# Early Sqrt table, identity on SyncE's queue, a first low part on VectorE, and a last tile squared and scaled in halves

## What is computed

```python
def _rmsnorm(x, g):
    xf = x.astype(jnp.float32)
    y = xf * lax.rsqrt(jnp.mean(xf * xf, axis=-1, keepdims=True) + EPS)
    return (y * g.astype(jnp.float32)).astype(x.dtype)
```

## Time and profile before

| | us |
|---|---|
| median of three runs (lowest, highest) | 1605.75 (1604.44, 1608.35) |
| the profiled execution | 1602.53 |
| its span (first to last instruction) | 1600.8 |

### The profile page before, as it was taken

How to read it: one execution, slowest core, us unless ns; L and a number is a source line. 1 busy time by engine, 2 the same in 40 slices (tenths; PEclk the granted TensorE clock), 3 DMA queues, 4 the chain that set the end, 5 groups by cost and what they waited for, 6 DMA issues and landing times.

```text
span 1600.8 us, 18917 instructions
## 1 busy us (share of the span) xinstructions
PE 1503.7 (94%) x7408; PEld 1009.0 (63%) x7409; DVE 662.9 (41%) x1092; ACT 512.8 (32%) x913; POOL 474.1 (30%) x250
## 2 busy tenths in 40 slices
PE   7999999999999999999998999899699998999996
PEld 6974567888788888888867766457334343433443
DVE  3156665223633333321135679573523233222234
ACT  5246566222543333321246333424111111111112
POOL 3441115444434444444424363432100000000000
PEclk9999999999999999999999999999799999999999
DMA  7333001232333233223223222217899999999995
GB/s 302 107 102 91 2 1 40 93 94 91 99 101 103 93 97 101 92 93 105 92 80 119 87 77 66 105 53 299 344 430 430 429 430 430 428 431 425 427 425 235
DMA packets 47272, 306.12 MB, mean 191 GB/s; under 512 B 6560, under 2 KB 6688, under 8 KB 33488
## 3 DMA queue, kind: packets, MB, share of 16 engines
q1 hardware_dynamic: 42256, 290.56, 47.1%
q0 software_dynamic: 4352, 12.25, 2.1%
q10 hardware_dynamic: 576, 2.10, 0.4%
HBM read 302.84 MB, written 4.19 MB: 192 GB/s over the span
## 4 chain that ended last, share of the span: by engine, by line
PE 74%; DMA 10%; DVE 9%; ACT 4%; issue 2%; POOL 0%; SPq 0%; DVEq 0%; ACTq 0%; POOLq 0%
PE banks L407 26%; PE banks L1090 11%; PE banks L437 10%; DMA ring<-experts 8%; PE banks L1121 4%; PE banks L2221 3%; PE banks L943 2%; PE banks L417 2%; PE banks L2150 2%; PE banks L1130 2%; PE banks L2166 2%; DMA arena<-experts 1%; PE banks L800 1%; PE banks L2133 1%; PE banks L801 1%
## 5 line engine op out<-in xcount | busy, mean ns | idle before, releaser
L370 POOL TENSOR_TENSOR arena_r<-ring,arena_r 128x1024 fp32r<-128x1024 f32 x143 | 352.2, 2468 | 444.5 <-ACT arena_r L355 444.5
L407 PE MATMUL banks<-hT_r,arena_r 128*128 128x512 f32 x1216 | 388.6, 391 | 5.5 <-POOL arena_r L370 4.3
L355 ACT ACTIVATE arena_r<-ring 128x1024 fp32r<-128x1024 f32 x143 | 150.6, 1059 | 461.3 <-PE banks L407 303.2
L407 PE MATMUL banks<-arena_r 128*128 128x512 f32 x800 | 291.7, 389 | 0.0
L407 PEld LDWEIGHTS banks<-hT_r,arena_r 128*128 128x128 f32 x1216 | 228.6, 188 | 59.5 <-issue 9.1
L1090 PE MATMUL banks<-ring,arena 128*64 128x512 f32 x720 | 223.3, 607 | 14.2 <-DMA ring<-experts 13.9
L437 PE MATMUL banks<-arena_r 128*128 128x512 f32 x784 | 184.1, 389 | 2.5 <-POOL arena_r L370 1.9
L407 PEld LDWEIGHTS banks<-arena_r 128*128 128x128 f32 x800 | 150.4, 188 | 31.0
L437 PEld LDWEIGHTS banks<-arena_r 128*128 128x128 f32 x784 | 147.0, 188 | 34.1 <-POOL arena_r L370 3.8
L1090 PEld LDWEIGHTS banks<-ring,arena 128*64 128x64 f32 x720 | 71.8, 140 | 149.5 <-issue 149.5
L1709 DVE TENSOR_TENSOR resid<-resid,banks 128x1024 f32<-128x1024 f32 x63 | 74.0, 1217 | 129.9 <-PE banks L1130 129.9
(11 more groups left out here) (443 smaller groups left out, 1896.6 us busy)
## 6 DMA issues: line engine op xcount, KB each, us to landing
arena<-experts SPq DMA_DIRECT2D x42, 2048.0 KB, 16.8
ring<-stream SPq DMA_DIRECT2D x162, 512.0 KB, 3.7
ring<-experts SPq DMA_DIRECT2D x37, 2048.0 KB, 16.5
ring<-experts SPq DMA_DIRECT2D x12, 1024.0 KB, 15.4
arena<-experts SPq DMA_DIRECT2D x12, 1024.0 KB, 16.7
ring<-experts SPq DMA_DIRECT2D x8, 512.0 KB, 12.3
resid<-x ACTq DMA_DIRECT2D x4, 512.0 KB, 5.6
grow<-grows POOLq DMA_DIRECT2D x4, 512.0 KB, 6.7
```

What stands on the lines that cost most here:

```text
L355: nc.scalar.activation(parts(name, m)[:, 0, :], tile(tile_n), ACT.Copy).then_inc(S["w_high"], 1)
L370: nc.gpsimd.tensor_tensor(w[:, 1, :], tile(tile_n), plain(w[:, 0, :]), ALU.subtract).then_inc(S["w_low"], 1)
L407: last = nc.tensor.matmul(pb[:, bank, :], w[:, a, k * P:(k + 1) * P], b[:, k, :], start=(k == 0 and part == 0), stop=(k == ND - 1 and part ...
```

## The change

Six edits. (1) VectorE sets a column to 1 at once, and ScalarE, after its four DMA issues, takes a Sqrt of it into an unused column. (2) The identity and eps are loaded by SP, as its first DMA, and counted with x tile 0 (`x_in0` reaches 32); SP issues W0 after x tile 2 (was tile 1), and after x tile 3 first `cols`, then W1; GpSimd no longer issues either. (3) The low part of W0 is made by VectorE; GpSimd waits for it and goes on with W1. (4) At n1 and n2, the last tile's square is shared: ScalarE squares the first 512 columns, VectorE squares and sums the other 512 (with eps added), and the root takes VectorE's sum as its bias. (5) In `norm_scale` without a gain, so at n1, n2 and n3, the last tile's rows are scaled in two halves, and PE's transposes of that tile wait for the first half and then for the second. (6) The router's load counts in `cols_in` too, so the semaphores `ident_in` and `route_in` go, and `half_ss` and `norm_half` come.

```diff
@@ sync, expert_stream and its user
-            sp.dma_start(router, W[W_ROUTE, :, 0:36 * ND]).then_inc(S["route_in"], 16)
+            sp.dma_start(router, W[W_ROUTE, :, 0:36 * ND]).then_inc(S["cols_in"], 16)
...
-            dve.wait_ge(S["route_in"], 16)
+            dve.wait_ge(S["cols_in"], 32)
@@ sync
+            sp.dma_start(cst[:, 0:P + 1], csts[:, 0:P + 1]).then_inc(S["x_in0"], 16)
             for s in range(RING):
                 if s < 2:
-                    sp.wait_ge(S[f"x_in{1 + 2 * s}"], 16)
+                    sp.wait_ge(S[f"x_in{2 + s}"], 16)
+                if s == 1:
+                    sp.dma_start(colt[:, :], cols).then_inc(S["cols_in"], 16)
                 sp.dma_start(ring[:, slot(s), :], W[s, :, :]).then_inc(landed[slot(s)], 16)
@@ gpsimd
-            pool.dma_start(cst[:, 0:P + 1], csts[:, 0:P + 1]).then_inc(S["ident_in"], 16)
-            pool.dma_start(colt[:, :], cols).then_inc(S["cols_in"], 16)
             pool.wait_ge(S["x_in3"], 16)
...
-            low_pool(pool, "proj")
+            pool.wait_ge(S["w_low"], 1)
+            low_pool(pool, "proj", 1)
@@ helpers
+        def first_half_square(act, n, src):
+            at = RMS.index((n, NT - 1))
+            act.wait_ge(S["rms_ss"], at)
+            nc.scalar.activation(junk[:, 0:512], src[:, 0:512], ACT.Square, scale=1.0 / D ** 0.5,
+                                 accum_out=rms_columns(n, NT - 1)[0]).then_inc(S["rms_ss"], 1)
+        def second_half_square(dve, src, spare):
+            nc.vector.tensor_tensor_reduce(out=spare[:, NT - 1, 512:D], in0=src[:, 512:D], in1=src[:, 512:D], scale=1.0 / D,
+                                           scalar=EPS, op0=ALU.mult, op1=ALU.add, accum_out=second_mean).then_inc(S["half_ss"], 1)
+        def shared_root(act, n):
+            mean, rt, rstd = rms_columns(n, NT - 1)
+            act.wait_ge(S["rms_ss"], RMS.index((n, NT - 1)) + 1)
+            act.wait_ge(S["half_ss"], SHARED.index(n) + 1)
+            nc.scalar.activation(rt, mean, ACT.Sqrt, bias=second_mean).then_inc(S["rms_rt"], 1)
@@ norm_scale
-                ins = nc.vector.tensor_scalar(dst[:, i, :], X[:, i, :], rstd, None, ALU.mult)
+                first = 0
+                if i == NT - 1:
+                    nc.vector.tensor_scalar(dst[:, i, 0:512], X[:, i, 0:512], rstd, None, ALU.mult).then_inc(S["norm_half"], 1)
+                    first = 512
+                ins = nc.vector.tensor_scalar(dst[:, i, first:D], X[:, i, first:D], rstd, None, ALU.mult)
@@ tr_pe
-                if ready is not None and b == 0:
+                if ready is not None and a == A - 1 and b == 0:
+                    pe.wait_ge(S["norm_half"], before // A + 1)
+                elif ready is not None and b == (B // 2 if a == A - 1 else 0):
                     pe.wait_ge(ready, before + a + 1)
@@ tensor
-            pe.wait_ge(S["ident_in"], 16)
+            pe.wait_ge(S["x_in0"], 32)
@@ scalar
-            act.wait_ge(S["ident_in"], 16)
+            act.wait_ge(S["dve_chain"], 1)
+            nc.scalar.activation(st[:, 449:450], st[:, 448:449], ACT.Sqrt)
             for i in range(NT):
-                act.wait_ge(S[f"x_in{i}"], 16)
+                act.wait_ge(S[f"x_in{i}"], 16 if i else 32)
+                if i == NT - 1:
+                    first_half_square(act, "n1", X[:, i, :])
+                    shared_root(act, "n1")
+                    continue
                 square(act, "n1", i, X[:, i, :])
                 root(act, "n1", i)
@@ scalar, n2: the same for i == NT - 1, behind act.wait_ge(S["post_x"], i + 1)
...
@@ vector
+            L(nc.vector.memset(st[:, 448:449], 1.0))
             for i in range(NT):
+                if i == NT - 1:
+                    dve.wait_ge(S["x_in3"], 16)
+                    second_half_square(dve, X[:, i, :], xn)
                 norm_scale(dve, chain, "n1", i)
+            first_weight = parts("proj", 0)
+            dve.wait_ge(S["w_high"], 1)
+            nc.vector.tensor_tensor(first_weight[:, 1, :], tile(W_PROJ_FM), plain(first_weight[:, 0, :]), ALU.subtract)\
+                .then_inc(S["w_low"], 1)
             dve.wait_ge(S["cols_in"], 16)
@@ vector, n2
+                if i == NT - 1:
+                    dve.wait_ge(S["post_x"], NT)
+                    second_half_square(dve, X[:, i, :], xn2)
                 norm_scale(dve, chain, "n2", i)
```

More of the change, by code:

```diff
@@ L142 @@
 SLOPES = [2.0 ** (-(h + 1)) for h in range(HEADS)]
-SEMS = """p3_prod rms_ss rms_rt norm_xn post_mm post_g post_x turned copied_dve copied_act
-w_used w_high w_low rows_low hT_low nsa_hi nsa_lo mla_hi mla_lo mask_in at_rinv at_b at_r at_rc at_acc h_high h_back cols_in ident_in x_in0 x_in1 x_in2 x_in3 tab_in g_in decay_in out_st
+SEMS = """p3_prod rms_ss rms_rt half_ss norm_half norm_xn post_mm post_g post_x turned copied_dve copied_act
+w_used w_high w_low rows_low hT_low nsa_hi nsa_lo mla_hi mla_lo mask_in at_rinv at_b at_r at_rc at_acc h_high h_back cols_in x_in0 x_in1 x_in2 x_in3 tab_in g_in decay_in out_st
 dve_chain proj_fm_ev proj_mla_ev proj_v_ev cmp_blocks cmp_gelu cmp_kv cmp_ready mla_stat mla_func mla_norm mla_tr mla_tr_ev mla_up mla_dve mla_act q_rope shift_in qk_in cs_pe cs_act cs_dve at_s at_max at_exp at_tr at_ev_dve at_ev_act at_pv at_o mg_sig mg_ev up_conv up_dve
@@ L150 @@
 over_ready x_tr x_ev_dve x_ev_act ex_gate ex_up ex_down ex_sig ex_hid h_tr h_ev y_hi y_lo spread p_ready placed placed_first added
-xg_in idx_in lg_done route_in
+xg_in idx_in lg_done
 spare_in at_in at_out gathers moe_x fin_y""".split()
@@ L163 @@
     + [(n, i) for n in ("n4", "n5") for i in range(NT)]
+SHARED = ("n1", "n2")
 SPLIT_TURNS = ("n1", "n2", "x2", "n3")
@@ L237, in rms_columns @@
             return [st[:, base + 4 * q:base + 4 * q + 1] for q in range(3)]
+        second_mean = st[:, 12:13]
         sums = st[:, 16:112].rearrange("p (w h) -> p w h", w=12)
@@ L2405, in _ @@
                     act.wait_ge(S["post_x"], i + 1)
+                    if i == NT - 1:
+                        first_half_square(act, n, X[:, i, :])
+                        shared_root(act, n)
+                        continue
                     square(act, n, i, X[:, i, :])
```

## The result

The changed kernel takes 1609.13 us (median of 12 runs, 1606.72 to 1612.55) against 1605.45 us of the kernel before in the same comparison (12 runs, 1603.87 to 1608.35): ratio 1.0022, 95% interval 1.0013 to 1.0031. It is slower by about 3.7 us, less than the 0.3% that I had called distinguishable, but well outside zero; the forecast was 0.55 us faster. The profiled execution took 1607.64 with a span of 1605.8, 5.0 us more than the span of before.

A forecast was written before the change was run, and what follows sets the result against it. PE ended last in 74% of the chain, with a ScalarE chain bounding the first 16 us. Front gain 1.35 less 0.8 for the clock, nothing at n2 and n3: 1605.75 - 0.55 = 1605.2 us, range 1601.2 to 1608.2.

The forecast's parts named there:

- The time of the transfers: Front loads: W0, cols, W1 (1.40 MB) follow x at 0.41 MB/us; W1 in at 12.5, bounds 11.6 and 13.9.
- the half rate: Front loads: GpSimd's own loads, issued at 8.1, were assumed to take half the transfer rate from 10.4.
- Rival 2: Front: cols landing at 14.7 hold ScalarE's weight copies, PE starts at 18.3; plus 1.8 us, 1607.5 us; chance 0.15.
- My sign of being wrong: PE gap before tile 3 at n2, first matmul after 16.5, or a difference of several us.
- The clock: Front: 2.5 us of PE idleness drops matmuls to 0.50; costs 0.8 us, bounds 0 and 1.6.
- rival 5: Front: transposes don't raise PE's clock, so longer idleness costs nothing; 1604.4 us, chance 0.02.
- The table and the identity: Start: both table loads leave ScalarE's chain; squares start at 4.65 instead of 6.15, transposes at 7.1 instead of 10.04.
- VectorE's half: n1, tile 3's shared square: ScalarE waits 0.8 us for VectorE, hidden as long as the weights land later.
- First low part on VectorE: Front: W0's low part takes 1.23 us on VectorE, bounds 1.23 and 4.7, removing the GpSimd path (16.42).
- n2 and n3: Later norms: nothing gained or lost, since PE's queue of transposes at the lower clock covers tile 3.
- Rival 3: n2: the clock doesn't fall, PE stands for tile 3, 0.63 us gained; 1603.8 us, chance 0.11.
- The range: Whole kernel: 1601.2 (all gains, half the spread) to 1608.2 us (cols late, some of the clock's price); chance within 0.92.

The follow-up runs named there:

- a_changed_again: The changed kernel itself, unaltered, run once more on another chip (also called "again"); ratio to the kernel before 1.0025.
- e2: Changed kernel, but GpSimd issues its four loads (1.5 MB) only when W1 has landed, not x tile 3; ratio to the kernel before 1.0010.
- e3: Changed kernel with n1's last transpose done 44 times instead of once, to keep PE busy; ratio to the kernel before 1.0011.
- e9: Changed kernel with cols behind W1 on SP's queue and ScalarE's wait for cols behind its two weight copies; ratio to the kernel before 1.0016.
- e1: Changed kernel with loads as before: cols on GpSimd's queue, W0 after x tile 1, W1 after x tile 3; 1604.22 us, ratio to the kernel before 0.9993.
- e4: Kernel before plus only the early dummy Sqrt and the identity issued by SP with its own signal; ratio to the kernel before 1.0000.
- e10: e8 with 10 repeats at n1, W1 issued after x tile 2 and GpSimd's loads after W1's landing; 1600.47 us, ratio to the kernel before 0.9975.
- e12: e10 with tile 3's square at n1 whole on ScalarE, n2's still shared; 1600.74 us, ratio to the kernel before 0.9969.
- e8: e6 with PE's n2 transposes reordered: tiles 0 to 2 early, 18 repeats of one transpose, tile 3 last; 1599.97 us, ratio to the kernel before 0.9965.
- e7: e8 with tile 3's square at n2 whole on ScalarE, the halves of the scaling kept; 1602.53 us, ratio to the kernel before 0.9975.
- e6: e1 with n1's last transpose done 14 times instead of once; 1603.18 us, ratio to the kernel before 0.9985.

## Why the prediction was wrong

**The time of the transfers, the term that failed.** I had W1 in at 12.5, with bounds 11.6 and 13.9; it landed at 16.6 and 17.0, though it was issued at 9.26, when the kernel before issued it too (9.30). The rate in 1 us bins, after:

```profile
GB/s 0 20 161 348 439 406 430 328 102 299 272 272 362 386 405 419 389 409 422 418 414 418 426 426 418 410 422 426 422 422 377 66 16 0 193 324 8 0 0 57
```

My sum ran at 0.41 MB/us without a hole from 7.7 on. The bins show a slower start (161 and 348 where the earlier trace rows has 229 and 360), so x tile 3 landed at 8.9 and not 8.1; then a hole in bin 8 (102), because W0 is issued only when x tile 2 has landed (7.66) and its data had barely begun when x ran out; then 299, 272 and 272 until 12. So in 8 to 12 the engines moved 0.95 MB where I had counted 1.6, and before 1.23. The runs bear the reason out: the five profiled executions with W0 issued at x tile 2 (changed, again, e2, e3, e9) have 102 to 156 GB/s in bin 8, the other nine, with W0 at x tile 1, 401 to 434. I had seen such a hole in the earlier trace rows (bins 10 and 11), and took it as a bound for one dip, though the change makes SP wait longer and so makes the hole itself. And I gave cols "10.3 to 11"; it landed at 13.9, having taken 5.0 us. From there the half rate was right: in 11.0 to 16.6 SP's queue moved 1.03 MB and GpSimd's 1.05 MB. The fit of the Trainium skill that the prediction sets beside its sum ("DMA: Bandwidth & Descriptors", section "Anatomy of one DMA") is given there for one DMA on GpSimd's path; W1, on SP's queue and beside GpSimd's loads, took 7.35 us where it gives 3.2.

**Rival 2 was the one that came.** Its mechanism (ScalarE's weight copies wait for cols and W1), its side (slower) and its points (cols later than 12.9, W1 later than 13.9) were right. My sign of being wrong came with it (a first matmul after 16.5), and so did a difference of several us, of which I had said that nothing in the first 16 us can give it: the late start and the clock behind it gave 5.45 by the landmark. The price of 1.8 us was too small (2.78), since it put W1 in by the time of cols' copy. Its chance, 0.15, followed from the transfer sum above.

**The clock.** It fell, as the idleness made likely, but I had 2.5 us of idleness and the late W1 made it 6.0. The bounds of its price were nothing and one stretch of 3.2 us at 0.50, 1.6; here 5.8 us of matmuls ran at 0.50, and it cost 2.67. With the idleness that I had assumed, the runs show either 1.60 (e1) or 0 (e4), so 0.8 was the middle of two outcomes and no run's own. That it rises under transposes alone holds here too: rival 5 falls again, since at n2 of the changed kernel the clock goes from 0.50 to 1.00 at about 448.3, amid the transposes, and e3's 44 repeats kept it at 1.00.

**The table and the identity: right.** One load, at 2.66; squares from 5.13 (I had 4.65; x tile 0 landed later), transposes from 7.81 (7.1). Root 3 at 11.05 to 11.34; I had its end at 11.0. All thirteen profiled executions with the identity on SP's queue start their squares at 4.73 to 5.30, where x tile 0 was in at 4.62 before; whether the identity beside x does this isn't shown. ScalarE waited 1.11 us for VectorE's half (I had 0.8 us against the whole square; e10 and e12 give 0.60), and this was hidden as said, by cols.

**First low part on VectorE: right in its cost** (1.22, I had 1.23), and it hides. The other bound, 4.7, took a mean that mixes six instructions of 2.75 us with two of 1.2; GpSimd stood still beside this one. GpSimd's path, which it removes, would not have been last here: W1's copy came later.

**n2 and n3: right.** 6.26 against 6.24, nothing gained; e8 and e7 show that PE's queue was the cover, and that the shared square is worth 0.38 us without it. Rival 3 didn't come: PE's transposes there ran at 0.50 in the changed kernel's profile as well.

**The range** (1601.2 to 1608.2) did not hold 1609.13, because both terms were bounded by a single row each and its top joined rival 2's 1607.5 with only some of the clock's price, though a late W1 and a fallen clock come together: in all four executions with 4.5 us of idleness or more (changed, again, e2, e9) it fell. 1607.5 with the 1.40 to 2.67 of the changed kernel's two executions would have been 1609 to 1610. That the range was missed by only 0.9 us owes something to the medians: they differ by 3.7 us where the landmarks of the two profiled executions are 5.45 apart.

## What to carry to other kernels

When an engine's chain is shortened, first ask when its inputs land. Here 1.7 us of ScalarE's work became 0.4 us for PE even with the loads unmoved (e4), and moving loads to a later trigger to make room for the first ones left a hole in the transfers (102 GB/s for a microsecond) and, together with cols ahead of W1 and GpSimd's loads beside it, cost 2.8. Look also at what stands ahead of the awaited copy in the program's order alone: PE's first matmuls didn't need W1. Before a last tile is split to have it sooner, look at what the consumer does at that moment: if it is busy without a gap (25 transposes in 4.60 us), the split is worth nothing until its queue is put in another order (e7 and e8, 0.38 us for the shared square). And a start that is moved forward without the work behind it makes PE idle longer, which can cost more than the move gives: add the clock to the sum together with the wait.

## What the runs showed of the hardware

Idle stretches of PE before the first matmul and the granted clock behind them: eight from 0.40 to 1.44 us held 1.00 (seven of them behind repeated transposes); 2.47 held (e4); 2.41 fell (e1); 4.52, 5.83, 6.01 and 6.03 fell. The two in the middle differ the other way round than their lengths, and in e1 the clock fell when PE had been at work for over a microsecond. The price went with the time that matmuls ran at 0.50: 1.4 to 1.6 us for 3.0 to 3.4 us in four executions and 2.67 us for 5.8 us in one. In all seven executions with repeated transposes ahead of the first matmul the clock was at 1.00 behind it; that the repeats kept it there in e6, where it fell in e1, rests on one execution of each.

In the changed kernel SP's and GpSimd's queues, both full, shared the engines evenly (1.03 and 1.05 MB in 5.6 us), whatever was urgent in one of them: the 512 KB of W1 took 7.35 us from issue to landing (7.9 in a_changed_again, 8.5 in e3), 5.8 in e2 with GpSimd's loads behind them, and 3.9 us in e1 and 3.8 before, where cols was not ahead of them in the queue.
